# The chunk inverses of an RWKV-7 stage, worked as 64-blocks on the two partition halves

## What is computed

```python
def rwkv7_scan(r, w, k, v, a_, b_):
    def step(state, inp):
        r_t, w_t, k_t, v_t, a_t, b_t = inp
        sa = jnp.einsum('bhvk,bhk->bhv', state, a_t)
        state = (state * w_t[:, :, None, :] + sa[..., None] * b_t[:, :, None, :]
                 + v_t[..., None] * k_t[:, :, None, :])
        return state, jnp.einsum('bhvk,bhk->bhv', state, r_t)
...
    kk = kk / jnp.maximum(jnp.sqrt(jnp.sum(kk * kk, axis=-1, keepdims=True)), 1e-12)
...
    y = (y - mean) * lax.rsqrt(var + GN_EPS) * ln_g.astype(f32).reshape(H, N) + ln_b.astype(f32).reshape(H, N)
```

## Time and profile before

| | us |
|---|---|
| three runs | 2408.09, 2416.16, 2421.20 |
| median | 2416.16 |
| the profiled execution, its own time | 2416.59 |
| its span, first to last instruction | 2414.8 |
| the four pairs' fronts, levels and joins together | 268.4 |

### The profile page before, as it was taken

One profiled execution on the slowest core, in us unless ns is written; L12 is line 12 of the kernel. 1 busy time (PEld: TensorE's weight loads), 2 busy tenths in 40 slices (PEclk: granted clock), 3 DMA queues, 4 the chain that ended last, 5 costly groups with the idle time before them and its releaser, 6 DMA issues. The chain is left out here.

```text
span 2414.8 us, 25286 instructions
## 1 busy us (share of the span) xinstructions
PE 2127.0 (88%) x10248; PEld 1198.0 (50%) x10248; DVE 731.0 (30%) x1337; ACT 391.0 (16%) x734; POOL 33.5 (1%) x80
## 2 busy tenths in 40 slices
PE   3999989699779999999579998978987999999964
PEld 2445888454454444443234488845445444444322
DVE  2244653442441111111234464434244111111103
ACT  2112110341310000000022211034131000000000
POOL 1000000000000000000100000000000000000001
PEclk8999998799889999999879999989988999999996
DMA  3400000220139999999750000021004899999983
GB/s 129 168 0 1 1 1 1 111 105 0 40 135 411 428 429 428 427 429 427 288 210 1 0 1 1 1 111 66 39 0 174 362 428 428 429 429 427 429 331 143
DMA packets 47357, 481.36 MB, mean 199 GB/s; under 512 B 7136, under 2 KB 7904, under 8 KB 19488
## 3 DMA queue, kind: packets, MB, share of 16 engines
q1 hardware_dynamic: 44960, 471.65, 46.7%
q0 software_dynamic: 2304, 8.39, 1.0%
HBM read 461.14 MB, written 18.87 MB: 199 GB/s over the span
## 5 line engine op out<-in xcount | busy, mean ns | idle before, releaser
L1696 PE MATMUL bank<-ring,hT 128*64 128x512 f32 x2048 | 456.7, 594 | 23.4 <-DMA ring<-in_we 20.1
L1696 PEld LDWEIGHTS bank<-ring,hT 128*64 128x64 f32 x2048 | 145.9, 137 | 322.7 <-issue 281.6
L684 PE MATMUL bank<-hT,ring 128*128 128x512 f32 (+1 forms) x608 | 269.5, 604 | 1.9 <-DVE hT L408 1.9
L1703 PE MATMUL bank<-ring,arena 128*64 128x512 f32 x1040 | 244.7, 613 | 16.8 <-DVE arena L1875 15.9
L1689 PE MATMUL bank<-arena 128*128 128x256 f32 x1024 | 251.4, 391 | 6.7 <-DVE arena L1716 6.7
L1689 PEld LDWEIGHTS bank<-arena 128*128 128x128 f32 x1024 | 188.9, 193 | 75.9 <-issue 47.1
L1875 DVE TENSOR_TENSOR arena<-arena,bank 128x256 f32<-128x256 f32 x64 | 27.0, 421 | 571.3 <-ACT arena L1817 570.8
L684 PEld LDWEIGHTS bank<-hT,ring 128*128 128x128 f32 (+1 forms) x608 | 116.2, 193 | 151.2 <-issue 148.9
L1815 ACT ACTIVATE arena<-bank 128x512 f32<-128x512 f32 x64 | 38.2, 597 | 799.8 <-PE bank L1696 799.8
L1703 PEld LDWEIGHTS bank<-ring,arena 128*64 128x64 f32 x1040 | 72.8, 140 | 152.1 <-issue 150.9
L1402 PE MATMUL bank<-hT,ring 128*128 128x512 f32 x256 | 110.3, 593 | 2.9 <-PEq L96 2.9
(11 more groups left out here) (399 smaller groups left out, 2192.2 us busy)
## 6 DMA issues: line engine op xcount, KB each, us to landing
ring<-in_we SPq DMA_DIRECT2D x195, 2048.0 KB, 21.2
expert_rows<-arena SPq DMA_DIRECT2D x128, 128.0 KB, 18.5
ring<-in_w_in SPq DMA_DIRECT2D x6, 2048.0 KB, 16.7
ring<-in_w_out SPq DMA_DIRECT2D x4, 2048.0 KB, 9.8
ring<-in_wm SPq DMA_DIRECT2D x2, 2048.0 KB, 16.3
ring<-in_w_in SPq DMA_DIRECT2D x2, 1920.0 KB, 7.8
ring<-in_w_in SPq DMA_DIRECT2D x2, 1664.0 KB, 24.4
ring<-in_w_in SPq DMA_DIRECT2D x2, 1152.0 KB, 26.8
```

Source lines behind the costliest of these rows:

```text
L684: last = nc.tensor.matmul(B[n % 4][0:w, :], ins_units[unit][:, k, u0:u0 + w], hT[:, k, :], start=k == 0, stop=k == KD - 1)
L1696: last = nc.tensor.matmul(bank[CAP * j:CAP * j + CAP, :], x[:, k, :], up_w(u, j, k), start=k == 0, stop=k == KD - 1)
L1703: last = nc.tensor.matmul(bank[CAP * half:CAP * half + CAP, :], hid[u][:, m, :], down_w(u, m, half), start=m == 0, stop=m == HM - 1)
```

## The change

- *Levels.* A is no longer 128x128 for the levels. Its two diagonal 64-blocks are worked by themselves: the block of tokens 0 to 63 on partitions 0 to 63, the other on partitions 64 to 127, as two matmuls with 64x64 weights, one on each half (`HALVES`). Only the odd columns are streamed, 32 instead of 128. Results lie packed: `T1c` 128x128 a quarter, `XUc` and `XLc` 128x256. There are five levels (L = 0 to 4), and then a join by products of 64x64 (`T1j`).
- *Front.* A goes to banks of its own and ScalarE copies it without a mask. The two heads of a `c` sit side by side: matmuls on partitions 0 to 63 and 64 to 127 take turns. The masks cover three products (128x384). The start is 128x256 for a chunk, made by GpSimd for the first and by VectorE for the second, and is turned by VectorE (`start_flip`), so that the transposes L792 and the copies L883 are gone. The transposes of `vT`, `BT`, `kT` come behind all products.
- *Sums.* `heads_summed` sums over a head with 32-column weights `head_pick` and 128 columns of data into four partition groups, `heads_given` brings the factors back with four matmuls of 512 columns. Root and reciprocal are now on 128x128 and change places. In the group norm the first gate comes before `heads_given` and the other three behind.
- *Setup.* GpSimd makes `lvl` and `pair` by way of `arena`, copies them and `eye` to the halves, and makes `head_pick`.

```diff
             def kk_sums():
                 eng.wait_ge(s_b2, 1)
                 eng.wait_ge(s_th, 4)
+                heads_summed(B[4], kk_sq).then_inc(s_bs, 1)
...
+            def heads_summed(bank, src):
+                for c in range(RC):
+                    for i in range(NT):
+                        last = nc.tensor.matmul(bank[32 * i:32 * i + 32, 0:P], head_pick[:, c, :],
+                                                src[:, c, i * P:(i + 1) * P], start=c == 0, stop=c == RC - 1)
+                return last
+            def heads_given(bank, c, src):
+                return nc.tensor.matmul(bank[:, :], head_give[:, c, :], src, start=True, stop=True)
...
+                                for e in range(2):
+                                    rows = slice(64 * e, 64 * e + 64)
+                                    last = nc.tensor.matmul(B[6 * s + e][:, c * P:(c + 1) * P], AT[rows, c, tok],
+                                                            BT[rows, c, tok], start=True, stop=True)
...
+                                for m, (lt, rt) in enumerate(((kT, AT), (BT, rT), (kT, rT))):
+                                    for e in range(2):
...
-                                for h in range(4):
-                                    last = nc.tensor.matmul(B[q][m, h * P:(h + 1) * P],
-                                                            big[q // 2][:, 4 * (q % 2) + h, 0, m],
-                                                            quarter(XU, q)[:, h, :], start=True, stop=True)
+                                for i in range(4):
+                                    for R in HALVES:
+                                        last = nc.tensor.matmul(packed1(B[q][R, i * 32:(i + 1) * 32], L),
+                                                                big[q // 2][R, 4 * (q % 2) + i, 0, R],
+                                                                odd1(XUc[R, 4 * q + i, :], L), start=True, stop=True)
...
+                                for i in range(4):
+                                    for R in HALVES:
+                                        last = nc.tensor.matmul(B[4 + q][R, i * 32:(i + 1) * 32], XLc[R, 4 * q + i, :],
+                                                                T1c[R, 4 * q + i, :], start=True, stop=True)
                                 last.then_inc(s_u1, 1)
...
+                        for s in range(2):
+                            eng.wait_ge(s_xa, 24 * (n0 // 2) + 12 + 2 * (s + 1))
+                            for R in HALVES:
+                                last = eng.activation(XU[s][R, :, R.start:R.start + 32],
+                                                      XUc[R, RH * s:RH * s + RH, 0:32], ACT.Copy)
+                            last.then_inc(s_xe, 1)
...
+                                eng.tensor_tensor(quarter(T1c, q), four(B[q][:, 0:P]),
+                                                  lvl[:, L, :].unsqueeze(1).to_broadcast([P, 4, 32]),
+                                                  ALU.mult).then_inc(s_tm, 1)
```

More of the change, by code:

```diff
@@ L124, in build @@
         causal = sb("causal", [P, P])
-        pair1 = sb("pair1", [P, P])
-        lvl = sb("lvl", [P, 6, 64])
+        pair = sb("pair", [P, 32])
+        eye = sb("eye", [P, 64])
+        lvl = sb("lvl", [P, 5, 32])
         scan_keep = sb("scan_keep", [P, SEQ])
+        head_pick = sb("head_pick", [P, RC, 32])
         slot_iota = sb("slot_iota", [P, SEQ])
@@ L414, in head_sums, with root_by_tile @@
                                         [:, :, 0], start=True, stop=True)
+            head_give = ring[:, 5, 1536:2048].rearrange("p (c n) -> p c n", c=RC)
+            def heads_summed(bank, src):
+                for c in range(RC):
+                    for i in range(NT):
[4 more added lines that the diff above has]
+                return nc.tensor.matmul(bank[:, :], head_give[:, c, :], src, start=True, stop=True)
+            def root_by_tile(eng, out, src):
+                for i in range(NT):
+                    rows = slice(32 * i, 32 * i + 32)
+                    last = eng.activation(out[rows, i * P:(i + 1) * P], src[rows, :], ACT.Sqrt)
+                return last
             def head_spread(out, src):
@@ L814, in _ @@
                                 eng.wait_ge(s_tm, levels + 4 * L + q + 1)
-                                if 1 <= L <= 4:
+                                if L:
                                     eng.wait_ge(s_xd, turned + 4 * (L - 1) + q + 1)
-                                else:
-                                    eng.wait_ge(s_xc, flips + 4 + (q + 1 if L else 0))
-                                for h in range(4):
-                                    last = nc.tensor.matmul(B[4 + q][m, h * P:(h + 1) * P],
-                                                            quarter(XL, q)[m, h, m],
-                                                            quarter(T1, q)[m, h, :], start=True, stop=True)
@@ new lines, in _ @@
+                        for q in range(4):
+                            eng.wait_ge(s_tm, levels + 20 + q + 1)
+                            eng.wait_ge(s_xc, flips + q + 1)
+                            for i in range(4):
+                                last = nc.tensor.matmul(B[4 + q][0:64, i * 64:(i + 1) * 64], XLc[0:64, 4 * q + i, :],
+                                                        T1j[0:64, 4 * q + i, :], start=True, stop=True)
+                            last.then_inc(s_u1, 1)
+                        if n0 == 0:
+                            eng.wait_ge(s_xz, 1)
@@ L876, in _ @@
                             eng.wait_ge(s_y, n0)
+                        for s in range(2):
+                            eng.wait_ge(s_a0, n0 + s + 1)
+                            for e in range(2):
+                                eng.activation(big[s].rearrange("p (c two) m t -> p two c m t", two=2)[:, e, :, 0, :],
+                                               four(B[6 * s + e][:, :]), ACT.Copy).then_inc(s_am, 1)
                         for i in range(3 * n0, 3 * n0 + 6):
@@ L932, in _ @@
                                 eng.wait_ge(s_t1, k)
-                                eng.tensor_tensor(odd4(quarter(T1, q)[m], L), odd4(four(B[q][m, :]), L),
-                                                  lvl[m, L, :].rearrange("p (a j) -> p a j", j=2 << L)
-                                                  .unsqueeze(1).to_broadcast(shape), ALU.mult).then_inc(s_tm, 1)
+                                eng.tensor_tensor(quarter(T1c, q), four(B[q][:, 0:P]),
+                                                  lvl[:, L, :].unsqueeze(1).to_broadcast([P, 4, 32]),
+                                                  ALU.mult).then_inc(s_tm, 1)
@@ L942, in _ @@
+                                for R in HALVES:
+                                    last = eng.tensor_tensor(
+                                        XU[q // 2][R, 4 * (q % 2):4 * (q % 2) + 4, R.start + 32:R.stop],
+                                        four(B[4 + q][R, 0:P]), quarter(XUc, q)[R, :, 32:64], ALU.add)
+                                last.then_inc(s_xa, 1)
                             if L < 4:
                                 turn_blocks(3)
+                        for q in range(4):
+                            k += 1
+                            eng.wait_ge(s_t1, k)
+                            eng.tensor_copy(quarter(T1j, q)[0:64], four(B[q][0:64, 0:256])).then_inc(s_tm, 1)
@@ L944, in _ @@
+                        for q in range(4):
+                            eng.wait_ge(s_u1, k - 3 + q)
+                            eng.tensor_copy(XU[q // 2][0:64, 4 * (q % 2):4 * (q % 2) + 4, 64:128],
+                                            four(B[4 + q][0:64, 0:256])).then_inc(s_xa, 1)
                         for s in range(2):
@@ L994, in _ @@
                                          stop=True).then_inc(s_gg, 1)
+                    gate(0)
+                    eng.wait_ge(s_gn5, 1)
+                    for c in range(RC):
+                        heads_given(B[4 + c], c, gn_rs).then_inc(s_gn7, 1)
+                    for c in range(1, RC):
+                        gate(c)
                 @block.scalar
```

255 lines of the change are left out of this document (153 added, 102 removed).

## The result

The changed kernel takes 2313.8 us (median of four runs, 2302.42 to 2317.08), the kernel before 2418.52 beside it (2408.09 to 2421.2): a ratio of 0.9544, 95% interval 0.9517 to 0.957. Six more runs of it, later and beside other kernels, gave 2308.4 us and 0.9536. The forecast was 2283, in a range from 2262 to 2375: the sign and the range held, and the gain was 31 us smaller than forecast. The profiled execution took 2313.70 us.

What follows compares the result with a forecast made beforehand. TensorE was taken to set the pace in the levels and the join. From 2416.6 us, 121.2 for the four pairs, 6.5 for `kk` and 8 for the group norm came off, 2.1 for setup on: 2283, range 2262 to 2375.

Steps and rivals of the forecast that it cites:

- Levels: Ten steps of each pair of chunks: 0.060 us a pair of records, 19.2 us in place of 36.
- Front: Start of each pair of chunks: products side by side, ended by ScalarE's copies, 12.3 us in place of 20.9.
- Join: Last stage of the inverses in each pair of chunks: 5.3 us, before 9.96.
- The clock, weighed against the rows: TensorE in the levels: expected to keep the high clock, as it stayed at 2.4 through L820 and L827.
- Tails: Work behind each join: no change in the forecast, 102.1 us for four.
- rival 1: Clock falls in all levels: a pair of records twice 0.060 us, 2411 us in all; chance 0.12 in full.
- its partial form: Clock falls in some pairs' levels or late in each: about 2340 us; chance 0.16.
- Rival 2: In the levels the two halves take turns: 0.116 us a pair of records, 2355 us in all; chance 0.06.
- Rival 3: In the levels halves take turns and the clock falls: 0.232 us a pair, 2529 us; chance 0.06 with the like.
- Sums and setup: Head sums: 6.5 us less in `kk`, 8 less in the group norm; setup 2.1 us more, once.

Runs made afterwards that it cites:

- the repeated kernel: The changed kernel itself, unedited, timed again beside later runs: 2308.4 us, 0.9536 of the kernel before.
- the run with 64 columns: Changed kernel with the first product of every level taking all 64 columns instead of the 32 odd ones: 2302.06 us, 0.9507 of the kernel before.
- the fastest version: Changed kernel plus full-row join, 64-column first products, reordered front and tail, both start blocks by GpSimd: 2262.95 us, 0.935 of the kernel before.
- the full-row kernel: Changed kernel with the join's products contracting over 128 rows, half of the moving side zero: 2277.37 us, 0.9415 of the kernel before.

## Why the prediction held, and where it was off

**Levels: right.** 18.8 to 19.2 us against 19.2, 0.058 to 0.059 us a pair against 0.060, TensorE without a gap, VectorE at 15.20 of 18.78 us and waiting 0.17 for each quarter's bank. The row taken for the price, L846, has outputs that go to the two halves of the partitions in turns, as the levels have. Its 128 rows are all in use, so what takes turns there is the outputs. The prediction read it for halves of the rows as well; for the levels the outputs' turns are enough, since with all operands on one row half they took 18.79 us too. That the price held is in part luck: the row was like the levels in the one feature that this run shows to suffice, and the prediction had not singled it out.

**Front: right in mechanism, 1 us short.** 13.3 against 12.3, ended by ScalarE's copies as said. The products side by side took 0.90 us for 16 records, as said too. The timeline of ScalarE in the kernel after:

```profile
241.08 1.09 ACT L972 ACTIVATE ring<-bank 128x512 f32<-128x512 f32 x2 [3.04 <-PE bank L830]
242.91 1.08 ACT L977 ACTIVATE hT<-bank 128x512 f32<-128x512 f32 x2 [0.74 <-PE bank L852]
```

A for the second tile is copied at 7.6 to 8.7 us of the front, where "until about 7.8" was said: the products had small waits for VectorE's masks in them.

**Join: the step that failed.** The forecast had 5.3. With the clock up the join takes 5.47 us (third pair of the repeated kernel), and that nearness is luck: the quarters take 0.95 each instead of 0.70 (12 records, not the 16 that the prediction counted, since a transpose is one), and the wait of 0.6 us ahead of them isn't there. The rest, to the 7.6 that it took on average, is the clock. The step that failed is in "The clock, weighed against the rows": it asked only whether the levels, with their few columns, would lose the clock, and took L820's 64x64 tiles as witness that such tiles keep it. L820 is one tile at a time on 64 rows too, but has 128 columns and 3.6 us; the join's new products have 64 columns, and 5.5 us of them. Which of the two made the difference no run shows. The join was not weighed at all.

**Tails: priced at nothing, cost 13.5 us.** The prediction touched them under rival 1 alone (8 to 10 us). The low clock that begins in the join runs into the tail until 291.8 and slows products that the change never touched, 5.8 us in the first pair. With the join on full rows that tail is back at 21.65 and the kernel at 2276 to 2277 us, 6 below the forecast. That it comes below is luck of the same kind: the tails before had the clock down in part (0.65 in the second, 0.81 in the fourth) and took 102.1 us, and with full rows and 64 columns they take 89.4. Join and tails together are 23 of the 31 us missing; the fronts are 4, and 7 are spread over the rest (3.3 of them in the experts of the second layer, L1814 to L2129, 559.6 us for 556.4, with the same instructions). These 3.3 belong to that one execution and not to the change: in the repeated kernel the same stretch takes 556.5. What the other 4 are no run has settled.

**Rival 1, and its partial form.** The prediction gave the levels' fall 0.16 in part and 0.12 in full. In the changed kernel's two profiled executions it did not occur, but it does occur: of 28 pairs with 32 columns in the levels, over seven profiled kernels, 6 ran them at half clock (32 to 35 us), all second pairs of a layer; of 24 with 64 columns in the first product, none. That points to the thin columns, but with six cases it is not shown: 20 of the 24 also had the full-row join, and what stands ahead of a second pair may have its part.

**Rival 2.** By the rule of the Trainium skill (TensorEngine Tiling (Array Packing), Restrictions and Gotchas, Gotcha 1: PSUM Pressure) the two halves could not write one bank at a time. The levels' pairs write one bank and take 0.058 us instead of this rival's 0.116, so the time it gave, 2355, is refuted. For two row halves that write one bank at once the run with 64 columns speaks: a pair on the two halves took 0.060 us there, and one tile alone needs 0.058 for a record of 64 columns (L896). Its outputs went to different partitions of the bank, and for that case the measurement decides against the rule as it is written; for the same partitions no run tests it. **Rival 3** needed 0.155 a pair.

**Sums and setup.** `kk` -6.5 as said: L431 took 1.08 us where 0.9 and 0.3 for the change of shape was forecast, and L718 behind it 7.13 in the first layer, where before it was 8.81; the fall behind two-column products is gone. The group norm gave 10.7 instead of 8, since the first layer's block, 29.3 us before, began with the clock down (its last line); the second layer's went from 26.8 to 22.7. Setup 2.6 for 2.1. Undoing the sums on the fastest version cost 15.9 us, some of it the clock.

## What to carry to other kernels

When products are cut into smaller tiles, weigh the clock for every stretch that gets thinner, the short ones behind the large one too: here some 5 us of 64x64 products, one at a time, cost 23 of the 31 us by which the forecast missed. Look then at work of nearly the same time that fills more of the array; multiplying by zeros on the idle rows cost 0.2 us a join (5.66 for 5.47) and gave back 31 to 36 us. And of a pattern that runs fast, change one feature at a time before naming the one that makes it fast.

## What the runs showed of the hardware that was not expected

- Products of 64 moving columns cost what 32 cost: 1.89 to 1.91 us for a step of 64 records, when outputs go to the two partition halves in turns. In groups of eight records for one half they cost 0.033 to 0.037 us each instead of 0.029.
- In the join's second step, where one 64x64 tile takes all products, records follow each other at 0.058 us, twice as long as in the levels (L896 at full clock: 29 in 1.78 us, with the change of shape behind them), and with 128 rows at 0.058 as well (32 in 1.96, 269.26 to 271.22 in the full-row kernel). What the full rows cost is the overlap shown above: the first of the second step's products no longer run beside the last of the first step's. Turns between output halves in the join might win up to 1 us a pair in its second step, an estimate from these two paces; this wasn't tried.
- The same instructions, with the same waits, lost the clock in one pair and kept it in another (7.83 and 5.47 us). What decides between them no run shows.
- The clock, once lost in the levels, stayed low for all their 29.7 us with TensorE busy throughout.
